# Block two of a two-block transformer: the first delta-rule chunk begun between dense products, and rotary embedding, blanks and decayed queries made by GpSimd

## The chip, the core and the metric

The kernel runs as one program on one core of a Trainium2 chip. The core has five engines that run side by side and wait for each other with semaphores: TensorE (PE: matmuls and transposes, into eight PSUM banks), VectorE (DVE), ScalarE (ACT), GpSimd (POOL) and SyncE (SP: here it only issues loads). The metric is the device time of one execution in microseconds (us); lower is better.

## The reference, cut to what matters

Two transformer blocks follow each other on 256 tokens of width 1024, all in float32. The change is in the second, whose mixer puts 16 meta tokens ahead of the 256 and runs two kinds of heads on one input projection:

```
proj = u @ w_in
dq, dk, dv, dz, db, da, aq, ak, av = split(proj)
# delta heads: 4 of width 128, forward and backward over the tokens
q, k, v = silu(short_conv([dq, dk, dv])); q, k = l2_norm(q) * 128**-0.5, l2_norm(k)
kk = k @ k.T ; a_low = strictly_lower(kk * decay * beta)
u, w = solve(a_low + I, [v * beta, k * beta * exp(gc)])
v_new = u - w @ S ; o = (q * exp(gc)) @ S + (q @ k.T * decay) @ v_new
S = S * g_last + k_dec.T @ v_new                # from chunk to chunk
# axial heads: 8 query heads on 2 key heads, width 64
q, k = rms_norm(aq) * q_norm, rms_norm(ak) * k_norm
x1, x2 -> x1 * cos - x2 * sin, x2 * cos + x1 * sin     # rotary embedding
o_at = softmax(q @ k.T / 8) @ av
mix = [rms_norm(o) * silu(dz), o_at] @ w_out
```

Then come a residual, a norm and an MLP. The reference's chunk of 64 is cut here into chunks of 16 (meta) and 128 tokens, which gives the same result.

## The kernel before

Every engine runs one long program, written out by Python in the order of the code; there is no scheduler and no loop on the chip. The order in which the functions `..._tensor`, `..._scalar`, `..._vector` and `..._gpsimd` call their operations is the order on that engine's queue, and the first instruction of a queue that waits holds back everything behind it. `then_inc(*vec.up(name))` tells that a result is there, `wait_ge(*vec.at(name))` waits for it.

**Dense products.** A weight chunk lands in a ring, ScalarE rounds it to a high part (`round_weights`, L515), VectorE subtracts for the low part (`lower_weights`, L521), and TensorE multiplies in three passes (L527 to L529). The input projection of block two is eleven such chunks, IN2 to IN2 + 10; the last four are `aq0`, `aq1` (queries of the axial heads), `z0`, `z1` (the gate dz), 48 matmuls each. This stage is called "two" (`in_tensor`, `in_scalar`, `in_vector`, `in_gpsimd`). `rows_tensor` and `rows_scalar` turn k (0) and v (1) of the delta heads to token order (`kv_tok`).

**Delta chunks.** A chunk is (d, t): direction d, token tile t, where t = 2 is the 16 meta tokens and t = 0, 1 are 128 tokens each. Six chunks run: (0,2), (1,2), (0,0), (1,1) from the start and (0,1), (1,0) from round 4. Each is a Python generator on each of three engines, and its steps are: sums of the gates ("gc"); the differences of their running sums ("R", which gives `d_a`, `d_qk` and `d_qdec`); k times k ("K", into `d_a`); the transpose of `d_a` and the first guess of its inverse `d_x`; then, for 128 tokens, six levels of two steps each that double the inverse (`d_w` from L2443, `d_x` from L2455 and L2457); and the products with q, v and the state S (names with `_last` are the buffers of (0,1) and (1,0), with `_meta` those of the meta chunks). One round of `beside_axial` takes one step of every chunk that lives and, between them, two steps (later one or two) of the axial heads.

**Rotary embedding.** The first steps of the axial heads prepare q and k of the token tiles t = 0, 1, 2: ScalarE squares (`sqk`, L2761), VectorE sums (L2818), ScalarE takes the root (L573, L575), VectorE scales and turns (`rotate_vector`, L2818 to L2847: 11 or 12 operations a tile into `rot`), TensorE transposes (L2710, L2714), ScalarE copies to `aT` and `akT`. After tile 2 the attention of the axial heads follows unit by unit.

**Dummy products.** `keep_running(e, n, ...)` puts n matmuls of the identity (L582) on TensorE's queue, whose result nobody reads.

## Time and profile before

| | us |
|---|---|
| median of 3 runs (lowest, highest) | 1154.88 (1152.62, 1156.89) |
| the profiled execution: device time | 1154.68 |
| the profiled execution: span from first to last instruction | 1152.9 |
| TensorE busy over the span | 1095.7 |
| VectorE busy | 761.2 |
| ScalarE busy | 608.9 |
| GpSimd busy | 65.5 |

The span is 1.8 us shorter than the device time of the same execution. "Busy" counts instructions in flight, so a busy TensorE can still be running at half its clock. The delta stage and the tail of stage "two" lie between 770 and 935 us of the span. A row of the timeline gives start, duration and count; of several instructions in a row the starts are closer together than the single duration, since the engine begins the next before the last has drained.

### The profile page before, as it was taken

How to read it: one execution, taken by the hardware profiler on the slowest of the kernel's cores; microseconds unless marked ns; L12 is line 12 of the kernel's file. 1: busy time of each engine (PE TensorE's matmuls, PEld its weight loads, DVE VectorE, ACT ScalarE, POOL GpSimd, SP SyncE). 2: the span in 40 equal slices, each digit the busy share in tenths (PEclk: the TensorE clock that was granted, in tenths of full speed). 3: DMA queues.
4: the chain of work that ended last, by engine and by line, in shares of the span. 5: the costliest groups of instructions: out<-in, count | busy, mean ns of one | idle time of the engine just before them, and what ended most of it. 6: DMA issues, size and time to landing. Idle time of an engine off the chain costs nothing.

```text
span 1152.9 us, 20471 instructions
## 1 busy us (share of the span) xinstructions
PE 1095.7 (95%) x8417; PEld 974.4 (85%) x8417; DVE 761.2 (66%) x1282; ACT 608.9 (53%) x1102; POOL 65.5 (6%) x84
## 2 busy tenths in 40 slices
PE   6999989999999999889999999998789999999997
PEld 3989567999899899879999988998668888999986
DVE  1786877899987775578655447874876557444443
ACT  2544756543544556656455555466664345565453
POOL 0012770000000000000000000110000000000000
PEclk8999999999999999999999999999789999999999
DMA  9997116899997354336856551250000045555540
GB/s 371 406 395 319 38 43 250 308 362 358 343 355 264 139 209 165 113 126 213 328 188 219 183 182 40 99 231 2 1 2 21 5 180 184 194 188 183 183 147 36
DMA packets 33564, 218.30 MB, mean 189 GB/s; under 512 B 4528, under 2 KB 5296, under 8 KB 8896
## 3 DMA queue, kind: packets, MB, share of 16 engines
q1 hardware_dynamic: 33472, 217.00, 50.9%
q8 instruction: 67, 1.10, 0.4%
q14 instruction: 25, 0.20, 0.0%
HBM read 215.93 MB, written 1.05 MB: 188 GB/s over the span
## 4 chain that ended last, share of the span: by engine, by line
PE 76%; DVE 11%; ACT 7%; DMA 2%; POOL 2%; issue 1%; DVEq 0%; SPq 0%; ACTq 0%
PE bank L527 20%; PE bank L529 20%; PE bank L528 20%; DVE low L521 2%; ACT high L515 2%; DMA ring<-ada_halves 2%; POOL zb L1141 1%; PE bank L567 1%; PE bank L644 1%; PE bank L2455 1%; PE bank L2457 1%; DVE y_tmp L1607 1%; PE bank L582 1%; PE bank L2443 1%; DVE stats L1609 1%
## 5 line engine op out<-in xcount | busy, mean ns | idle before, releaser
L521 DVE TENSOR_TENSOR low<-ring,high 128x2048 fp32r<-128x2048 f32 (+1 forms) x139 | 317.6, 2287 | 242.2 <-ACT high L515 241.8
L515 ACT ACTIVATE high<-ring 128x2048 fp32r<-128x2048 f32 (+1 forms) x139 | 264.7, 1906 | 247.5 <-PE bank L529 199.5
L527 PE MATMUL bank<-act_high,high 128*128 128x256 f32 (+1 forms) x1072 | 308.3, 288 | 0.0
L529 PE MATMUL bank<-act_high,low 128*128 128x256 f32 (+1 forms) x1072 | 303.8, 283 | 0.0
L528 PE MATMUL bank<-act_low,high 128*128 128x256 f32 (+1 forms) x1072 | 303.6, 283 | 0.0
L527 PE MATMUL bank<-high,act_high 128*128 128x512 f32 (+1 forms) x632 | 233.7, 370 | 3.2 <-DVE act_low L3005 1.8
L529 PE MATMUL bank<-high,act_low 128*128 128x512 f32 (+1 forms) x632 | 231.2, 366 | 0.0
L528 PE MATMUL bank<-low,act_high 128*128 128x512 f32 (+1 forms) x632 | 231.2, 366 | 0.0
L527 PEld LDWEIGHTS bank<-act_high,high 128*128 128x128 f32 x1072 | 205.0, 191 | 4.5 <-issue 2.4
L528 PEld LDWEIGHTS bank<-act_low,high 128*128 128x128 f32 x1072 | 205.0, 191 | 2.4 <-issue 1.4
L529 PEld LDWEIGHTS bank<-act_high,low 128*128 128x128 f32 x1072 | 204.9, 191 | 0.0
L527 PEld LDWEIGHTS bank<-high,act_high 128*128 128x128 f32 x632 | 119.5, 189 | 23.8 <-DVE act_low L3005 2.0
L529 PEld LDWEIGHTS bank<-high,act_low 128*128 128x128 f32 x632 | 119.2, 189 | 20.6
L528 PEld LDWEIGHTS bank<-low,act_high 128*128 128x128 f32 x632 | 119.4, 189 | 18.0
L626 DVE SCALAR_TENSOR_TENSOR ada_acc<-ring,c_act,ada_acc 128x512 f32<-128x512 f32 x105 | 79.4, 756 | 4.6
L1134 ACT ACTIVATE zb<-zb,ust 128x128 f32<-128x128 f32 x80 | 35.5, 446 | 27.1 <-DVE ust L1126 27.1
L582 PEld LDWEIGHTS bank<-cols 128*128 128x128 f32 x338 | 41.2, 200 | 4.9 <-issue 4.8
L582 PE MATMUL bank<-cols 128*128 128x128 f32 x338 | 43.3, 285 | 0.0
L1141 POOL TENSOR_SCALAR zb<-zb,ust 128x128 f32<-128x128 f32 (+1 forms) x48 | 40.2, 851 | 32.5 <-DVE ust L1414 24.7
L2352 POOL MEMSET conv<- 128x24 f32 x1 | 0.1, 123 | 538.8 <-DVE x_tok L2122 538.8
L1149 PE MATMUL bank<-cols,zb 128*128 128x128 f32 x96 | 16.4, 281 | 7.9 <-DVE zb L1954 2.4
L1149 PEld LDWEIGHTS bank<-cols,zb 128*128 128x128 f32 x96 | 10.6, 141 | 14.2 <-DVE zb L1954 2.6
(511 smaller groups left out, 1384.1 us busy)
## 6 DMA issues: line engine op xcount, KB each, us to landing
ring<-chunks SPq DMA_DIRECT2D x138, 1024.0 KB, 5.0
ring<-ada_halves SPq DMA_DIRECT2D x38, 1024.0 KB, 5.1
o_land<-ada_halves SPq DMA_DIRECT2D x6, 1024.0 KB, 11.9
ring<-raw_cmp SPq DMA_DIRECT2D x4, 1024.0 KB, 11.5
x_tok<-ada_halves SPq DMA_DIRECT2D x3, 1024.0 KB, 15.1
gate_rows<-ada_b SPq DMA_DIRECT2D x4, 512.0 KB, 9.9
bias<-bias_by_distance SPq DMA_DIRECT2D x1, 2048.0 KB, 13.2
ln_rows<-ln_g SPq DMA_DIRECT2D x4, 512.0 KB, 6.0
```

Of the source, the lines that this page charges most:

```text
L515: e.activation(weights(c)[0], in_ring(("w", c)), ACT.Copy).then_inc(*act.up("high", c))
L521: e.tensor_tensor(low, in_ring(("w", c)), high.bitcast(F32), ALU.subtract).then_inc(*vec.up("low", c))
L527: e.matmul(out_, ah, bh, start=start, stop=False)
L528: e.matmul(out_, ah, bl, start=False, stop=False)
L529: return e.matmul(out_, al, bh, start=False, stop=stop)
L567: last = e.matmul(out_, src[:, k, toks], w[:, k, c0:c0 + n_cols], start=k == 0, stop=k == n - 1)
L582: m = e.matmul(b[:, 0:P], ident, ident, start=True, stop=True)
L626: e.scalar_tensor_tensor(acc, w_[:, k, :], c_, acc, ALU.mult, ALU.add).then_inc(*vec.up("ada_op", l, j, i))
L644: m = e.matmul(b[:, i:i + 1], acc[:, i * P:(i + 1) * P], ones[:, 0:1], start=True, stop=True)
L1134: x = e.activation(z[:, c], z[:, c], ACT.Exp, bias=st[:, t:t + 1], scale=-1.0, accum_out=st[:, 2 + t:3 + t])
L1141: x = e.tensor_scalar(z[:, c], z[:, c], st[:, 4 + t:5 + t], None, ALU.mult)
L1149: m = e.transpose(b[:, tok(i)], z[:, tok(i)], ident)
```

## The change

- **First chunk ahead.** The generators of chunk (0,0) are made before stage "two" (`ahead`) and take their first four steps inside it: gc after `aq0`, R and K after `aq1`, the transpose of `d_a` after `z0`. `beside_axial` then goes on with step 5 of (0,0) in its round 0. On TensorE the turn of v (`rows_tensor(e, 1)`) moves behind `z1`; on ScalarE its copies (`rows_scalar(e, 1)`) move to the end of the stage, behind the table load.
- **Rotary embedding.** `rotate_vector` keeps the sum of the squares; the other operations of a tile go to GpSimd (`rotate_gpsimd`). The square and the sum of tile t + 1 are drawn forward to the fourth axial step of tile t, behind the end of tile t's rotation.
- **Blanks and decayed queries.** The `memset` of a quarter of `d_xT` and the product `d_qdec` times q of the four 128-token chunks leave VectorE for GpSimd.
- **Dummy products.** 20 ahead of tile 1's transposes are dropped; 12 in the first level of (0,2) become 6.

```diff
@@ in_tensor
-            for half in range(2):
-                rows_product(e, IN2 + 7 + half, f"aq{half}")
+            rows_product(e, IN2 + 7, "aq0")
+            steps_of(ahead, 1)
+            rows_product(e, IN2 + 8, "aq1")
+            steps_of(ahead, 2)
             rows_product(e, IN2 + 9, "z0")
             rows_tensor(e, 0)
+            steps_of(ahead, 1)
+            rows_product(e, IN2 + 10, "z1")
             rows_tensor(e, 1)
-            rows_product(e, IN2 + 10, "z1")
@@ in_scalar
                 if half == 0:
                     rows_scalar(e, 0)
-                    rows_scalar(e, 1)
+                    steps_of(ahead, 1)
                     round_weights(e, OUT2)
+                    steps_of(axial, 2)
             e.preload_act_table_set(ROOTS)
-            steps_of(axial, 2)
+            rows_scalar(e, 1)
@@ in_vector
             lower_weights(e, IN2 + 9)
+            steps_of(ahead, 2)
             lower_weights(e, IN2 + 10)
+            steps_of(axial, 1)
+            steps_of(ahead, 1)
             steps_of(axial, 2)
+            steps_of(ahead, 1)
             lower_weights(e, OUT2)
-            steps_of(axial, 2)
+            steps_of(axial, 1)
@@ in_gpsimd
+            rotate_gpsimd(e, 0)
+            blank_gpsimd(e, 0, 0)
+            rotate_gpsimd(e, 1)
+            blank_gpsimd(e, 1, 1)
+            rotate_gpsimd(e, 2)
+            for d in range(2):
+                decay_gpsimd(e, d, d)
+            for d in range(2):
+                blank_gpsimd(e, d, 1 - d)
+            for d in range(2):
+                decay_gpsimd(e, d, 1 - d)
@@ delta_tensor
-                keep_running(e, 12, "x", k)
+                keep_running(e, 6, "x", k)
@@ delta_scalar
+            if k == (0, 0):
+                e.activation(B["qk"], B["qk"], ACT.Exp).then_inc(*act.up("qk", k))
...
-            if real:
+            if real and k != (0, 0):
                 e.activation(B["qk"], B["qk"], ACT.Exp).then_inc(*act.up("qk", k))
@@ axial_tensor
-                    if t == 1:
-                        keep_running(e, 20, "rot", t)
-                    e.wait_ge(*vec.at("rot", t))
+                    e.wait_ge(*pool.at("rot", t))
@@ rotate_gpsimd (was rotate_vector; in the new order)
+            e.wait_ge(*act.at("rot_square", t))
+            if t < 2:
+                e.tensor_tensor(x_[:, 0:8, :], x_[:, 0:8, :], qk_norm_row[0:r, 0:1, :].broadcast_to([r, 8, 64]), ALU.mult)...
+            e.tensor_tensor(k_, k_, qk_norm_row[0:r, 1:2, :].broadcast_to([r, 2, 64]), ALU.mult)...
+            e.wait_ge(*act.at("rot_root", t))
+            e.tensor_tensor(k_, k_, rst[0:r, 1, 8:10].unsqueeze(2).broadcast_to([r, 2, 64]), ALU.mult)...
+            e.wait_ge(*vec.at("rot_sum", t))
+            e.tensor_tensor(tmp, hi_, sin, ALU.mult)...
+            e.tensor_tensor(tmp2, lo_, sin, ALU.mult)...
+            e.tensor_tensor(o_lo, lo_, cos, ALU.mult)...
+            e.tensor_tensor(o_hi, hi_, cos, ALU.mult)...
+            e.tensor_tensor(o_lo, o_lo, tmp, ALU.subtract)...
+            e.tensor_tensor(o_hi, o_hi, tmp2, ALU.add).then_inc(*pool.up("rot", t))
```

The three places below are where this shows in the order of the instructions; lines are those of each version's own file.

On VectorE, between the low part of `z1`'s weights (`low_61`) and the delta stage (its first row is `d_st` 16x4), before:

```order
L521 TENSOR_TENSOR low_61<-ring_55,high_59 128x2048 [waits scalar_two]
L2818 TENSOR_REDUCE rst<-sqk 128x10 [waits scalar_two]
L2820 TENSOR_TENSOR aqk<-aqk,qk_norm_row 128x512
...
L521 TENSOR_TENSOR low_62<-ring_56,high_60 128x2048 [waits scalar_two]
L2839 TENSOR_TENSOR rot<-aqk,rope 128x20x16 [waits vector_two]
...
L2847 TENSOR_TENSOR rot<-rot,sqk 128x20x16 [waits vector_two]
L2581 TENSOR_TENSOR d_st<-d_st 16x4 [waits scalar_delta,vector_two]
```

and now:

```order
L521 TENSOR_TENSOR low_61<-ring_55,high_59 128x2048 [waits scalar_two]
L2840 TENSOR_REDUCE rst<-sqk 128x10 [waits scalar_two]
L2625 SCALAR_TENSOR_TENSOR d_a<-bank,ba,d_a 128x128 [waits tensor_two,scalar_two]
...
L2631 TENSOR_TENSOR d_x<-d_a,masks 64x256 [waits vector_two]
...
L2636 TENSOR_TENSOR d_x<-d_aT,masks 64x256 [waits scalar_two]
...
L2639 TENSOR_TENSOR d_x<-masks,d_x 128x512 [waits vector_two]
L521 TENSOR_TENSOR low_62<-ring_56,high_60 128x2048 [waits scalar_two]
L2840 TENSOR_REDUCE rst<-sqk 128x10 [waits scalar_two]
L2607 TENSOR_TENSOR d_st<-d_st 16x4 [waits scalar_delta,vector_two]
```

The rotation is gone from the queue, chunk (0,0) has come into it, and the second sum (tile 1) stands ahead of the delta stage.

On ScalarE, from the copies of k (`kv_tok`) to the delta stage, before:

```order
L2186 ACTIVATE kv_tok<-bank 16x512 [waits tensor_two]
L2186 ACTIVATE kv_tok<-bank 128x512 [waits tensor_two] x2
L515 ACTIVATE high_60<-ring_56 128x2048 [waits tensor_two,in_ring1]
L2279 ACTIVATE z_tok<-bank 128x2x256 [waits tensor_two]
L2285 ACT_TABLE_LOAD
L2524 ACTIVATE d_st<-bank 16x4 [waits tensor_delta,scalar_two]
```

and now:

```order
L2567 ACTIVATE d_aT<-bank 128x512 [waits tensor_two]
L515 ACTIVATE high_60<-ring_56 128x2048 [waits tensor_two,in_ring1]
L2780 ACTIVATE sqk<-aqk 128x640 [waits gpsimd_two]
L2286 ACTIVATE z_tok<-bank 128x2x256 [waits tensor_two]
L2293 ACT_TABLE_LOAD
L2186 ACTIVATE kv_tok<-bank 16x512 [waits tensor_two]
L2186 ACTIVATE kv_tok<-bank 128x512 [waits tensor_two] x2
L2548 ACTIVATE d_st<-bank 16x4 [waits tensor_delta,scalar_two]
```

The copies of v now stand between the table load and the delta stage, and tile 1's square, which waits for GpSimd's rotation of tile 0, stands ahead of `z1`'s copy.

On TensorE, in round 2 of the delta stage around tile 1's transposes, before:

```order
L582 MATMUL bank<-cols 128x128 [waits scalar_delta]
L582 MATMUL bank<-cols 128x128 x19
L2710 MATMUL bank<-cols,rot 128x128 [waits vector_delta,scalar_delta]
...
L2714 MATMUL bank<-cols,rot 128x128 [waits vector_delta,scalar_delta]
L2424 MATMUL bank<-cT 128x128 [waits vector_two,scalar_delta]
...
L2430 MATMUL bank<-cols,d_a_meta 16x16 [waits vector_delta,scalar_delta]
```

and now:

```order
L2466 MATMUL bank<-d_x,d_aT 64x64 [waits vector_delta]
...
L2730 MATMUL bank<-cols,rot 128x128 [waits gpsimd_two,scalar_delta]
...
L2734 MATMUL bank<-cols,rot 128x128 [waits gpsimd_two,scalar_delta]
L2447 MATMUL bank<-cT 128x128 [waits vector_two,scalar_delta]
...
L2453 MATMUL bank<-cols,d_a_meta 16x16 [waits vector_delta]
```

The dummy products are gone, chunk (0,0) is already at its second level (L2466), and the transposes wait for GpSimd.

## Rows read from the trace of the kernel before

**Rows 1.** Five stretches: length; busy us of each engine; granted TensorE clock; DMA.

```profile
core 0: us, PE busy (x) PEld busy (x) DVE busy (x) ACT busy (x) POOL busy (x), PEclk, DMA share, GB/s
797.40:829.40 32.00, 21.16 (x203) 19.48 (x202) 26.15 (x90) 21.42 (x71) 0.00 (x0) 0.84 0.00 1
829.40:842.00 12.60, 12.53 (x155) 11.10 (x155) 6.53 (x28) 9.27 (x38) 0.00 (x0) 0.60 0.01 1
842.00:862.00 20.00, 14.51 (x275) 12.02 (x274) 15.77 (x51) 12.61 (x38) 0.00 (x0) 0.95 0.01 3
862.00:867.00 5.00, 5.00 (x78) 4.14 (x80) 3.06 (x11) 2.05 (x6) 0.00 (x0) 0.51 0.00 0
867.00:935.00 68.00, 67.44 (x1085) 59.49 (x1086) 37.47 (x91) 27.45 (x84) 0.00 (x0) 1.00 0.13 42
```

**Rows 2.** TensorE's timeline: start, us, line, operation, count, idle time before.

```profile
770.34 0.48 PE L527 MATMUL bank<-high,act_high 128*128 128x256 f32 x1
...
790.30 1.47 PE L2179 MATMUL bank<-cols,cT 128*16 128x128 f32 x12 [1.22 <-ACT cT L2242]
...
800.30 0.63 PE L2710 MATMUL bank<-cols,rot 128*128 128x128 f32 x4 [2.41 <-DVE rot L2847]
...
809.65 4.63 PE L582 MATMUL bank<-cols 128*128 128x128 f32 x40
816.92 0.63 PE L2710 MATMUL bank<-cols,rot 128*128 128x128 f32 x4 [2.64 <-DVE d_a_meta L2599]
...
817.49 1.06 PE L2424 MATMUL bank<-cT 128*128 128x128 f32 x8
...
872.62 1.15 PE L2443 MATMUL bank<-d_x,d_aT 64*64 64x64 f32 x32
```

**Rows 3.** VectorE's groups in 797.4 to 829.4: line, shapes, count, busy us, mean ns.

```profile
L2588 DVE SCALAR_TENSOR_TENSOR d_a<-bank,d_st,masks 128x128 f32<-128x128 f32 x8 | 2.6, 329 | 0.0
L2612 DVE TENSOR_TENSOR d_x<-d_aT,masks 64x256 f32<-64x256 f32 x4 | 1.7, 420 | 0.1
L2843 DVE TENSOR_TENSOR rot<-rot,sqk 128x320 f32<-128x320 f32 x2 | 1.0, 478 | 0.0
```

**Rows 4.** VectorE's timeline.

```profile
777.07 0.18 DVE L2343 TENSOR_TENSOR ba<-ba,ex_row 128x24 f32<-128x24 f32 x1
...
828.62 0.69 DVE L2615 TENSOR_TENSOR d_x<-masks,d_x 128x512 f32<-128x512 f32 x1
...
855.84 0.87 DVE L2612 TENSOR_TENSOR d_x_last<-d_aT_last,masks 64x256 f32<-64x256 f32 x2 [2.21 <-ACT d_aT_last L2541]
```

**Rows 5.** ScalarE's timeline.

```profile
784.62 0.74 ACT L2761 ACTIVATE sqk<-aqk 128x640 f32<-128x640 f32 x1
...
790.54 2.95 ACT L2186 ACTIVATE kv_tok<-bank 16x512 f32<-16x512 f32 x6
...
797.49 0.60 ACT L2279 ACTIVATE z_tok<-bank 128x512 f32<-128x512 f32 x1 [2.20 <-PE bank L529]
798.11 1.28 ACT L2285 ACT_TABLE_LOAD   x1
799.40 0.16 ACT L2524 ACTIVATE d_st<-bank 16x4 f32<-16x4 f32 x1
...
808.04 0.21 ACT L575 ACTIVATE rst<-rst 128x10 f32<-128x10 f32 x1
...
852.90 2.43 ACT L2519 ACTIVATE d_kdec<-kv_tok,d_st 128x128 f32<-128x128 f32 x8
```

**Rows 6.** Single lines: GpSimd's products and VectorE's low parts; ns min/median/max.

```profile
L1064 POOL TENSOR_TENSOR hid<-hid 128x120 f32<-128x120 f32 x1 | 0.4, 389 | 29.2 <-ACT hid L903 29.2
...
L1495 POOL TENSOR_TENSOR dbias<-bias,taken x8: 720/726/2697, 138.4 to 164.9; 128x256 f32<-128x256 f32 x8
...
L2357 POOL TENSOR_TENSOR conv<-cT x8: 640/642/2752, 738.5 to 755.9; 128x272 f32<-128x272 f32 x8
...
L521 DVE TENSOR_TENSOR low<-ring,high x11: 2279/2293/2574, 720.0 to 795.3; 128x2048 fp32r<-128x2048 f32 x11
```

More of the change, by code:

```diff
@@ L2187, in rows_scalar, with in_tensor @@
                     *act.up("kv_tok", kv, t))
-        def in_tensor(e, axial):
+        def in_tensor(e, axial, ahead):
             for t in range(QT):
@@ L2344, in in_vector @@
             lower_weights(e, IN2 + 9)
+            steps_of(ahead, 2)
             lower_weights(e, IN2 + 10)
+            steps_of(axial, 1)
+            steps_of(ahead, 1)
             steps_of(axial, 2)
+            steps_of(ahead, 1)
             lower_weights(e, OUT2)
-            steps_of(axial, 2)
+            steps_of(axial, 1)
         def in_gpsimd(e):
@@ L2466, in delta_tensor @@
                 e.wait_ge(*act.at("rows", k))
+                e.wait_ge(*pool.at("blank", k))
                 e.wait_ge(*vec.at("xT", k, n_levels - 1))
@@ L2605, in delta_vector @@
                 e.tensor_tensor(xs[r, 0:4, :], B["a"][r, :, r], level(0, 1 - back, r), ALU.mult).then_inc(*vec.up())
-            if real:
-                e.memset(B["xT"][far, :, near], 0.0).then_inc(*vec.up())
             if k == (0, 2):
@@ L2672, in program, with beside_axial @@
         CHUNKS = (((0, 2), 0), ((1, 2), 0), ((0, 0), 0), ((1, 1), 0), ((0, 1), 4), ((1, 0), 4))
-        def beside_axial(chunks, axial):
+        def beside_axial(chunks, axial, ahead):
             live, waiting, n = [], list(CHUNKS), 0
@@ L2678, in beside_axial @@
                 for k, start in [c for c in waiting if c[1] == n]:
-                    live.append(chunks(*k, k[1] == 2 or k[0] == k[1]))
+                    live.append(ahead if k == (0, 0) else chunks(*k, k[1] == 2 or k[0] == k[1]))
                 waiting = [c for c in waiting if c[1] > n]
@@ L2756, in axial_scalar, with square @@
         def axial_scalar(e):
+            def square(t):
+                r, h0 = TT_ROWS[t], 0 if t < 2 else 8
+                e.wait_ge(*(pool.at("rot", t - 1) if t else act.at("aq1")))
+                e.activation(sqk[0:r, h0:10, :], aqk[0:r, t, h0:10, :], ACT.Square).then_inc(*act.up("rot_square", t))
             for t in range(3):
-                r = TT_ROWS[t]
-                h0 = 0 if t < 2 else 8
-                e.wait_ge(*(vec.at("rot", t - 1) if t else act.at("aq1")))
-                e.activation(sqk[0:r, h0:10, :], aqk[0:r, t, h0:10, :], ACT.Square).then_inc(*act.up("rot_square", t))
+                r, h0 = TT_ROWS[t], 0 if t < 2 else 8
+                if t == 0:
+                    square(t)
                 yield
@@ L2766, in axial_scalar @@
                 yield
+                if t < 2:
+                    square(t + 1)
                 yield
@@ L2813, in rotate_vector, with blank_gpsimd, decay_gpsimd, rotate_gpsimd @@
             r, h0 = TT_ROWS[t], 0 if t < 2 else 8
+            e.wait_ge(*act.at("rot_square", t))
+            e.tensor_reduce(rst[0:r, 0, h0:10], sqk[0:r, h0:10, :], AX_X, ALU.add).then_inc(*vec.up("rot_sum", t))
+        def blank_gpsimd(e, d, t):
+            back = d
+            e.wait_ge(*pool.now())
+            e.wait_ge(*act.at("w", (d, t)))
+            e.memset(buf[d, t]["xT"][HALVES[1 - back], :, HALVES[back]], 0.0).then_inc(*pool.up("blank", (d, t)))
+        def decay_gpsimd(e, d, t):
+            B = buf[d, t]
+            e.wait_ge(*pool.now())
+            e.wait_ge(*act.at("qdec", (d, t)))
+            e.tensor_tensor(B["qdec"], B["qdec"], cT[:, 0:4, rows_of(t)], ALU.mult).then_inc(*pool.up("qdec", (d, t)))
+        def rotate_gpsimd(e, t):
+            r, h0 = TT_ROWS[t], 0 if t < 2 else 8
             x_, sq_ = aqk[0:r, t, h0:10, :], sqk[0:r, h0:10, :]
@@ L3036, in tensor @@
             pe.stage("two")
-            axial = axial_tensor(e)
-            in_tensor(e, axial)
+            axial, ahead = axial_tensor(e), delta_tensor(e, 0, 0, True)
+            in_tensor(e, axial, ahead)
             pe.stage("delta")
-            beside_axial(lambda *chunk: delta_tensor(e, *chunk), axial)
+            beside_axial(lambda *chunk: delta_tensor(e, *chunk), axial, ahead)
             pe.stage("end")
@@ L3062, in scalar @@
             act.stage("two")
-            axial = axial_scalar(e)
-            in_scalar(e, axial)
+            axial, ahead = axial_scalar(e), delta_scalar(e, 0, 0, True)
+            in_scalar(e, axial, ahead)
             e.wait_ge(*act.now())
             act.stage("delta")
-            beside_axial(lambda *chunk: delta_scalar(e, *chunk), axial)
+            beside_axial(lambda *chunk: delta_scalar(e, *chunk), axial, ahead)
             e.wait_ge(*act.now())
@@ L3092, in vector @@
             vec.stage("two")
-            axial = axial_vector(e)
-            in_vector(e, axial)
+            axial, ahead = axial_vector(e), delta_vector(e, 0, 0, True)
+            in_vector(e, axial, ahead)
             e.wait_ge(*vec.now())
             vec.stage("delta")
-            beside_axial(lambda *chunk: delta_vector(e, *chunk), axial)
+            beside_axial(lambda *chunk: delta_vector(e, *chunk), axial, ahead)
             e.wait_ge(*vec.now())
```

56 lines of the change are left out of this document (29 added, 27 removed).

## The prediction

> **What bounds the kernel now.** The page gives a busy TensorE for nearly the whole span, so the first thing to find is where it is not the limit. I read the windows first, stage by stage, then TensorE's timeline for the waits in them, then the queues of the engines that it waits for. From 867 to 935 us TensorE is busy 67.4 of 68.0 us at full clock: there the time is TensorE's work [rows 1]. From 797.4 to 829.4 it is different: TensorE counts as busy 21.2 of 32 us, and that includes 20 dummy products (4.6 us) and 12 more; VectorE is busy 26.2 us of the 32 [rows 1, 2]. TensorE waits there 2.4 us for tile 0's rotation (800.30) and 2.6 us ahead of tile 1's transposes (816.92) [rows 2]. So this stretch is VectorE's, and its end is the first guess of chunk (1,1), 828.62 + 0.69 = 829.3 [rows 4]. After it, up to 842, TensorE is the limit at mostly half its clock (0.60), and from 842 to 862 waits alternate with work: 14.5 of 20 us busy, with VectorE held 2.2 us by ScalarE at 855.84 [rows 1, 4]. The change works on the VectorE stretch, on that wait, and on the amount of work in TensorE's stretch.
>
> **What goes from VectorE.** In 797.4 to 829.4 the six products of a rotation take 1.0 us for two calls each (tiles 0 and 1), 5.9 us in all; tile 2 and the scalings of tiles 1 and 2 are some 2.5 more. Chunk (0,0)'s share in that stretch is half of the groups of `d_a`, `d_qk` and `d_x`: 4 of 8 at 0.33 for each of three kinds and 2 of 4 at 0.42 for each of two, 0.7 for the last, together 6.3 us [rows 3]. What comes in is two levels of (0,0), about 2.2 us. VectorE's 26.2 us become about 14, so it no longer sets the pace there. The blanks (64x256, below the 0.42 us of a product of that shape) and the decayed queries lie where TensorE is the limit or behind this slack; I give them nothing.
>
> **What it costs in stage "two".** `aq0` starts at 770.34; `z1`, a product of the same size, ran from 791.8 (790.30 + 1.47) to 797.4, where ScalarE's copy is let go, so a product takes some 5.7 us and `aq0` ends at 776.05 [rows 2, 5]. The gate sums behind it need `ba`, which VectorE ends at 777.25 [rows 4]: TensorE waits 1.3 us. Then, with matmuls at 1.06 us for eight instructions (817.49): gc 0.5, `aq1` 5.7, R and K 2.1, `z0` 5.7, the turn of k 1.5, the transpose 0.6 (as at 816.92), `z1` 5.7 [rows 2]. The end is 799.2 instead of 797.4: of the 4.5 us put in, 1.2 are paid by the wait at 790.30 that goes, and 1.5 by the turn of v that moves behind. Behind `z1` ScalarE now has its copy (0.6), the table load (1.28) and the three copies of v (half of 2.95) before the meta chunk may begin: 799.3 + 3.4 = 802.7, and 803.3 for ScalarE's first row of the delta stage, which was at 799.40 [rows 5]. The head thus starts **3.9 us later**.
>
> **GpSimd's price.** The trace has no rotation on GpSimd. Its two-input products of 120 and 256 columns take 0.39 and 0.72 us [rows 6]: 0.1 us plus 2.4 ns a column, so 0.88 us for 320 columns, 1.34 for 512, 0.41 for 128. Lower bound: the 0.64 us of 272 columns where both inputs are one tensor, 0.75 for 320. Upper bound: the longest row, 2.75 us, a product that met VectorE's low part [rows 6]. I take the fit, since no low part runs beside most of the products. A rotation is 1.8 us ahead of the root and 5.8 behind it. Tile 0: its square ended at 785.4 and moves with `aq1` by 1.6 us, so GpSimd begins at 787.0, beside a low part that runs to 789.2, and ends at 797 to 798. What waits for it first is tile 1's square, ahead of `z1`'s copy on ScalarE, and that copy can't start before 799.2: the rotation and the 0.7 us of the square are just covered. Tile 1: its root stood 8.8 us behind ScalarE's first row of the stage (799.40 to 808.25) [rows 5]; less one set of gate sums and the wait for VectorE, plus 1.2 us of copies for (0,0), I make it 7.4 us, 810.7. GpSimd ends at **816.5**. Nothing covers this one: the square of tile 2 waits for it on ScalarE, the sum behind that on VectorE, and the transposes with everything behind them on TensorE.
>
> **The new head.** From 816.5: transposes 0.9, K of (1,1) 1.1, its `d_a` 1.2 (four at 0.33 each, less overlap), the low part 2.3, the meta chunks' guesses 1.5 (six small operations of a quarter us, an estimate), one level of (0,0) 0.7, the first guess of (1,1) 2.5 [rows 2 to 4, 6]. This gives 826.7 against 829.3, **2.6 us earlier**. Against it stand the decayed queries: two products of 1.3 us that fall beside that first guess on the same operand ports, and a TensorE that may run at half clock there since the 20 dummies are gone. Both together cost between 0 and 3 us; I take 0.8, since most of the guess's operations are short. Term one: **-1.8**.
>
> **Behind the head.** At 852.90 ScalarE makes eight `d_kdec` copies (2.43 us) ahead of the transpose copy that VectorE waits for at 855.84 [rows 4, 5]. Four of them, (0,0)'s, are then long done: 1.2 us, and 0.3 for a blank on VectorE's side of the same chain. Term two: **-1.5** (0 to -2).
>
> In TensorE's stretch, (0,0) is four steps further, so two levels of it have left it. A level is 16 instructions for `d_w` (32 take 1.15 us at 872.62) and 32 for `d_x`, 1.6 us [rows 2]. Two are 3.2 us less work where TensorE is the limit; some of it will be lost to waits when fewer chunks live, so term three is **-2.6** (0 to -3.2).
>
> **Loads and queues.** No load is moved. The rounding of the two output weight chunks shifts by +2 and about -2 us, which shifts the loads that wait for their ring slots; DMA share is 0.00 to 0.13 there [rows 1], so that is hidden.
>
> **Sum.** -1.8 - 1.5 - 2.6 = -5.9 us. The profiled execution took 1154.7 us, 0.2 below the median of the runs shown, so the forecast is **1148.8 us**, 0.5% below that median, the size that a measurement of this kernel can just tell from no change.
>
> **Rivals.**
> 1. *GpSimd sets the pace of the head.* For: GpSimd's products of 272 columns are 0.64 us, but 2.75 us when one meets a low part, whose own longest is 2.57 instead of 2.29 [rows 6]; the six products read short runs of 16, which no row shows; nothing hides tile 1. Against: VectorE is mostly idle in 811 to 816. At the mean over the eight (1.17 us for 272 columns) the six products take 8.3 us instead of 5.3, with the scalings 3.8 us more; the head then gains nothing, and the time is 1148.8 + 3.8 = 1152.6. The Trainium skill, "SBUF — State Buffer", section "Who interferes with whom", says that a VectorE instruction with two SBUF inputs and a GpSimd instruction that reads SBUF exclude each other, the later one waiting for the whole of the other. The rows agree: 2752 against 640 ns, beside a low part of 2293.
> 2. *The clock holds better.* 829.4 to 842 and 862 to 867 are at 0.60 and 0.51 of the clock [rows 1], both behind idle time of TensorE that the change shortens; chunk (0,0)'s levels now fill the head. If 5 us of work at half clock run at full, another 3.5 us go: 1145.3. Against it: the dummies are gone.
> 3. *Slower: the clock is lost.* Of 32 dummy products 6 are left. Before, the 20 ran from 809.65 [rows 2] in the middle of a stretch at 0.84 [rows 1]. If TensorE is at half clock through the head and does not get the full one back between 842 and 862, its 14.5 us of work there become 29 in a stretch of 20: some 8 us more, and 3 in the head for transposes, R, K and their like. -5.9 + 11 = +5: 1160. It decides when more than 6 us of full-clock work turn to half clock; in the rows before, the full clock came back by itself at 842.
> 4. *Nothing comes of it.* The head gains what stage "two" lost, and the two levels taken out of the tail leave waits of the same length, as the last chunks (0,1) and (1,0) start in the same round as before: 1154.5. Against it: 67.4 of 68.0 us busy.
>
> **How the numbers follow.** Forecast 0.44 (own range 1146 to 1152, of which about half lies below the bound of 0.5%), rival 1 0.22, rival 2 0.20, rival 3 0.08, rival 4 0.06. Faster by over 0.5%: rival 2 and somewhat over half of the forecast, 0.46; slower by over 0.5%: most of rival 3 and the far end of rival 1 (both rotations late by 10 us or more), 0.10; the rest, 0.44, within it. The range that leaves out 2 in 10 reaches from the middle of rival 2 to beyond rival 4: 1143 to 1156.5.
>
> **What would show it.** In the changed trace: `z1` ends near 799.2 and ScalarE's first delta row stands near 803.3; GpSimd's products of 320 columns take 0.75 to 1.0 us; tile 1's rotation ends near 816.5 and the sum of tile 2 on VectorE right behind it; the first guess of (1,1) ends near 827.5; the stretch from there to the end of the delta stage is some 4 us shorter than the 105.7 us of before (829.3 to 935). The forecast is wrong in its core if tile 1's transposes wait for GpSimd beyond 820, or if the stage's granted clock is below that of before.

## The result and the profile after

The changed kernel takes **1148.36 us** (median of 4 runs, 1147.47 to 1150.43), the kernel before in the same comparison 1155.25 (1152.62 to 1156.89): a ratio of 0.9941, 95% interval 0.992 to 0.9962. A second comparison, run beside experiments 5 to 7, gave 1146.36 against 1153.97, 0.9927 (0.9908 to 0.9945). What was expected of it:

> The changed kernel once more, beside the others on one chip. Its runs so far spread over 3 us, and in the runs of all kernels the time falls by about 0.7 us for each 0.001 that the mean granted clock is higher. Theory (three terms, the head's worth less than forecast): 1147 to 1149, a ratio of 0.993 to 0.995, and about 7.5 us below the kernel before at the same granted clock. Rival (the first measurement was lucky): 1150 or more.

The change is faster by 0.6 to 0.7%. The forecast was 1148.8 us.

The page of the changed kernel gives VectorE 752.8 us (66%) instead of 761.2, and GpSimd 96.3 instead of 65.5. TensorE's sum moves only from 1095.7 to 1093.3. The five stretches of [rows 1], in the execution that was profiled (1150.43 us, span 1148.6, the slowest of the four):

```profile
core 0: us, PE busy (x) PEld busy (x) DVE busy (x) ACT busy (x) POOL busy (x), PEclk, DMA share, GB/s
797.40:829.40 32.00, 21.10 (x252) 19.04 (x250) 20.82 (x56) 22.39 (x73) 17.03 (x23) 0.77 0.00 1
829.40:842.00 12.60, 12.10 (x155) 10.54 (x155) 5.66 (x21) 8.10 (x34) 0.61 (x2) 0.64 0.01 3
842.00:862.00 20.00, 15.84 (x292) 12.83 (x292) 15.79 (x52) 11.45 (x34) 2.54 (x2) 0.92 0.01 2
862.00:867.00 5.00, 5.00 (x94) 4.54 (x92) 2.56 (x10) 2.43 (x7) 0.00 (x0) 0.62 0.02 3
867.00:935.00 68.00, 68.00 (x982) 59.71 (x978) 36.39 (x87) 27.69 (x85) 0.00 (x0) 0.97 0.19 63
```

In the first stretch VectorE has gone from 26.15 to 20.82 us and is no longer the engine that fills it; GpSimd has 17.03. The granted clock there is 0.77, where before had 0.84. GpSimd's timeline there (start, us, engine, line, operation; in brackets the idle time before it and what ended it):

```profile
787.78 3.03 POOL L2863 TENSOR_TENSOR aqk<-aqk,qk_norm_row 128x512 f32<-128x512 f32 x1 [29.74 <-ACT sqk L2780]
...
810.37 0.40 POOL L2868 TENSOR_TENSOR aqk<-aqk,rst 128x128 f32<-128x128 f32 x1 [8.09 <-ACT rst L575]
...
810.95 0.87 POOL L2879 TENSOR_TENSOR sqk<-aqk,rope 128x320 f32<-128x320 f32 x1
...
815.20 0.86 POOL L2887 TENSOR_TENSOR rot<-rot,sqk 128x320 f32<-128x320 f32 x1
...
825.49 2.73 POOL L2852 TENSOR_TENSOR d_qdec<-d_qdec,cT 128x512 f32<-128x512 f32 x2
```

TensorE's timeline of the same stretch:

```profile
803.00 0.19 PE L2434 MATMUL bank<-ba,masks 16*16 16x4 f32 x2 [2.43 <-ACT kv_tok L2186]
...
816.21 1.09 PE L2730 MATMUL bank<-cols,rot 128*128 128x128 f32 x4 [3.79 <-POOL rot L2887]
...
817.30 1.92 PE L2447 MATMUL bank<-cT 128*128 128x128 f32 x8
...
829.37 1.12 PE L2466 MATMUL bank<-d_x,d_aT 64*64 64x64 f32 x16 [3.65 <-DVE d_w_meta L2650]
```

And VectorE's: its last row on the gates, then the two guesses, and the last sum of the delta stage:

```profile
777.67 0.18 DVE L2351 TENSOR_TENSOR ba<-ba,ex_row 128x24 f32<-128x24 f32 x1
...
825.73 2.77 DVE L2636 TENSOR_TENSOR d_x<-d_aT,masks 64x256 f32<-64x256 f32 x2
828.53 0.69 DVE L2639 TENSOR_TENSOR d_x<-masks,d_x 128x512 f32<-128x512 f32 x1
...
854.58 0.87 DVE L2636 TENSOR_TENSOR d_x_last<-d_aT_last,masks 64x256 f32<-64x256 f32 x2 [1.31 <-ACT d_aT_last L2567]
...
930.91 0.69 DVE L2680 TENSOR_TENSOR o_acc<-o_acc,bank 128x512 f32<-128x512 f32 x1 [1.10 <-PE bank L2517]
```

The reader is to see three things. The rotation of tile 1 ends at 816.06 and TensorE goes on at 816.21, having waited 3.79 us for it. Then `L2636`, which took 0.87 us in [rows 4], takes 2.77, and it lies beside GpSimd's decays (825.49 to 828.22). Last, the first guess of (1,1) ends at 829.22, nearly where it did (829.31).

**A common clock for the comparison.** The gates end at another time in each execution (773.4 to 778.5 us over the kernels below), in code that the change does not touch. So all traces are compared from the start of VectorE's last row on the gates (777.67 above): "head" is from there to the end of the first guess of (1,1), "middle" to the end of the last first guess of the last chunks, "tail" to the end of the last `o_acc` sum. What is left after that is 217.0 us in every trace (216.98 to 217.10). Times are worked out from rows like those above.

| kernel | median us | ratio (95%) | head | middle | tail | tail's clock | tail's TensorE instructions |
|---|---|---|---|---|---|---|---|
| before | 1155.25 | 1 | 52.24 | 30.91 | 75.62 | 0.96 | 1188 |
| changed | 1148.36 | 0.9941 (0.992 to 0.9962) | 51.55 | 29.36 | 73.02 | 0.93 | 1092 |
| changed, again | 1146.36 | 0.9927 (0.9908 to 0.9945) | 52.03 | 28.51 | 68.73 | 1.00 | 1092 |
| 1 decays moved | 1147.56 | 0.9934 (0.9916 to 0.9952) | 49.72 | 29.37 | 73.01 | 0.93 | 1092 |
| 2 root early | 1148.00 | 0.9931 (0.991 to 0.9952) | 51.21 | 28.79 | 71.22 | 0.96 | 1092 |
| 3 GpSimd's part only | 1151.11 | 0.9966 (0.9949 to 0.9982) | 51.29 | 30.12 | 74.58 | 0.96 | 1188 |
| 4 chunk ahead only | 1150.00 | 0.9957 (0.9939 to 0.9976) | 52.22 | 29.75 | 70.13 | 0.98 | 1092 |
| 5 dummies back | 1147.08 | 0.9933 (0.9915 to 0.995) | 51.96 | 28.68 | 71.16 | 0.96 | 1092 |
| 6 three moves | 1144.30 | 0.9918 (0.99 to 0.9936) | 47.30 | 29.09 | 72.84 | 0.93 | 1092 |
| 6 again | 1144.20 | 0.9905 (0.9887 to 0.9923) | 47.31 | 29.22 | 72.90 | 0.93 | 1092 |
| 7 moves and dummies | 1143.79 | 0.9921 (0.9895 to 0.9947) | 47.29 | 28.86 | 72.61 | 0.98 | 1122 |
| 8 low part later | 1144.64 | 0.991 (0.9895 to 0.9926) | 45.53 | 30.50 | 72.93 | 0.93 | 1092 |

The tail of one and the same kernel is 73.02 us in one execution and 68.73 in another, at a granted clock of 0.93 and 1.00. Length times clock is the same within 1 us: 67.9 and 68.7 (the clock has two digits, so such a product is good to some 0.4 us). Read that way, the kernels with the chunk ahead have 67.7 to 68.7 us of full-clock tail, and those without it 72.6 (before) and 71.6 (experiment 3). Experiment 7 stands apart with 71.2, as 30 more instructions lie in its tail.

### The profile page after: what moved, and what is told of

Read it like the earlier page. It is cut to its first block, busy times and chain, and to the rows that moved or that the text cites. A ratio compares the mean times of both kernels' runs of the same rounds, so it can differ in the third digit from the quotient of the medians.

```text
span 1148.6 us, 20388 instructions
## 1 busy us (share of the span) xinstructions
PE 1093.3 (95%) x8365; PEld 973.4 (85%) x8365; DVE 752.8 (66%) x1246; ACT 609.1 (53%) x1102; POOL 96.3 (8%) x120
## 4 chain that ended last, share of the span: by engine, by line
PE 77%; DVE 9%; ACT 7%; DMA 2%; POOL 2%; issue 1%; DVEq 0%; SPq 0%; ACTq 0%; POOLq 0%
PE bank L527 20%; PE bank L529 20%; PE bank L528 20%; DVE low L521 2%; ACT high L515 2%; DMA ring<-ada_halves 2%; POOL zb L1141 1%; PE bank L567 1%; PE bank L2478 1%; PE bank L644 1%; PE bank L2480 1%; PE bank L582 1%; DVE y_tmp L1607 1%; DMA ring<-raw_ksv 1%; DVE stats L1609 1%
## 5 line engine op out<-in xcount | busy, mean ns | idle before, releaser
L582 PEld LDWEIGHTS bank<-cols 128*128 128x128 f32 x286 | 36.2, 206 | 4.3 <-issue 4.2
L582 PE MATMUL bank<-cols 128*128 128x128 f32 x286 | 38.2, 291 | 0.0
```

The lines of the kernel that those rows point to most:

```text
L582: m = e.matmul(b[:, 0:P], ident, ident, start=True, stop=True)
```

## The experiments

**1. The decays elsewhere.** GpSimd makes the decayed queries of (0,0) ahead of tile 1's rotation and those of (1,1) ahead of tile 2's.

```diff
             blank_gpsimd(e, 0, 0)
+            decay_gpsimd(e, 0, 0)
             rotate_gpsimd(e, 1)
             blank_gpsimd(e, 1, 1)
+            decay_gpsimd(e, 1, 1)
             rotate_gpsimd(e, 2)
-            for d in range(2):
-                decay_gpsimd(e, d, d)
```

> The changed kernel with the decayed queries of (0,0) made by GpSimd ahead of tile 1's rotation and those of (1,1) ahead of tile 2's, instead of behind tile 2's. Theory (port): the decays, two products in 2.73 us at 825.49, stretched VectorE's L2636 at 825.73 from 0.87 to 2.77 us; moved away, that row is 0.9 to 1.5 again, the first guess of (1,1) ends 1.9 us earlier than 829.2, TensorE's wait of 3.65 us ahead of it shrinks by as much, and the time is 1.9 below that of the changed kernel, 1146.5 (ratio to before 0.9925). Rival (clock): TensorE at half clock or another wait sets the place; the row is short but the next level starts no earlier, and the time stays at 1148.4. Second rival: the product of (0,0) now meets VectorE's low part at 798.5 and pushes tile 1's rotation beyond 816; the time is 1149 or more.

VectorE's timeline of that kernel, at the guess:

```profile
824.54 0.87 DVE L2636 TENSOR_TENSOR d_x<-d_aT,masks 64x256 f32<-64x256 f32 x2
825.45 0.69 DVE L2639 TENSOR_TENSOR d_x<-masks,d_x 128x512 f32<-128x512 f32 x1
```

and TensorE's row behind it:

```profile
826.29 1.12 PE L2466 MATMUL bank<-d_x,d_aT 64*64 64x64 f32 x16 [1.75 <-DVE d_w_meta L2650]
```

The row is 0.87 us again, the head is 49.72 instead of 51.55 (1.83 less; 2.3 less than in the second trace), and TensorE's wait has gone from 3.65 to 1.75. The middle is as long as in the changed kernel's first trace (29.37 and 29.36); head and middle together are 1.8 us shorter than there and 1.5 shorter than in the second, so the gain is kept: the port theory holds, and the two rivals fall. The Trainium skill, "SBUF — State Buffer", section "Who interferes with whom", has the rule: a VectorE instruction with two SBUF inputs and a GpSimd instruction that reads SBUF don't run together, and the later one waits for the whole of the other. The traces agree: 2.77 us beside the decays, 0.87 without. The time of the whole (1147.56 against 1148.36 and 1146.36) can't tell 1.9 us.

**2. Tile 1's root early.** `root` is the wait for the sum and the two operations of the root, taken out of `axial_scalar`.

```diff
@@ in_scalar
             rows_scalar(e, 1)
+            root(e, 1)
@@ axial_scalar
-                e.wait_ge(*vec.at("rot_sum", t))
-                rsqrt(e, rst[0:r, 1, h0:10], rst[0:r, 0, h0:10], 1.0 / 64, eps6, "rot_root", t)
+                if t != 1:
+                    root(e, t)
```

> The changed kernel with the root of tile 1 (two operations on ScalarE) right behind the copies of v, ahead of the delta stage, instead of at 809.77. Theory (nothing covers tile 1): GpSimd has waited 8.1 us for that root; its rotation of tile 1 now ends near 809 instead of 816.1, TensorE's wait of 3.8 us at 816.2 is gone, and K of (1,1) comes at about 815. VectorE then still stands at tile 2's sum until 816.7, as ScalarE's square of tile 2 is behind the rounding of an output chunk; so of the 7 us only 1.5 reach the first guess of (1,1): 827.7, and a time of 1146.9 (ratio 0.9928). Rival (clock): the rotation comes early, but the first guess of (1,1) stays at 829.2 because it waits for products at half clock; 1148.4. Second rival: all of it arrives, the first guess ends 4 us earlier, 1144.5.

ScalarE's timeline of that kernel around tile 2's square:

```profile
812.65 0.60 ACT L2564 ACTIVATE d_qdec<-bank 128x512 f32<-128x512 f32 x1 [2.40 <-DVE d_qk L2623]
813.14 0.62 ACT L2565 ACTIVATE d_a<-d_a 128x512 f32<-128x512 f32 x1
813.66 1.90 ACT L515 ACTIVATE high<-ring 128x2048 fp32r<-128x2048 f32 x1
815.46 0.29 ACT L2786 ACTIVATE sqk<-aqk 16x128 f32<-16x128 f32 x1
```

and VectorE's row that waits for it:

```profile
815.78 0.27 DVE L2846 TENSOR_REDUCE rst<-sqk 16x2 f32<-16x128 f32 x1 [2.62 <-ACT sqk L2786]
```

The rotation of tile 1 ended at 806.85, 9.2 us earlier (7 from the gates), and TensorE made the transposes at 811.48 without a wait. The head gained 0.3 us (0.8 against the second trace), less than the 1.5 expected. One wait of the head did go. In the changed kernel VectorE waited 1.47 us (1.19 in its second trace) for K of (1,1), which TensorE makes behind tile 1's transposes:

```profile
819.32 1.13 DVE L2625 SCALAR_TENSOR_TENSOR d_a<-bank,ba,d_a 128x128 f32<-128x128 f32 x4 [1.47 <-PE bank L2447]
```

In experiment 2 the same row has no wait:

```profile
816.88 1.10 DVE L2631 SCALAR_TENSOR_TENSOR d_a<-bank,ba,d_a 128x128 f32<-128x128 f32 x4
```

So the rotation held the head by 1.2 to 1.5 us, as expected. Ahead of that wait a second chain ran beside it, nearly as long: VectorE's `d_a` and `d_qk`, ScalarE's exponentials, the rounding of an output chunk (1.90 us), tile 2's square, tile 2's sum. This chain came later in experiment 2: the sum began 40.20 us behind the gates, instead of 39.01 and 39.76 in the changed kernel's two traces. The early rotation (801.18 to 806.85) now lies beside VectorE's small gate sums:

```profile
801.88 0.76 DVE L2613 TENSOR_TENSOR d_st<-d_st 16x4 f32<-16x4 f32 x1 [2.50 <-ACT d_st L2556]
803.00 0.46 DVE L2615 TENSOR_TENSOR d_st<-d_st,ba 16x4 f32<-16x4 f32 x1 [0.37 <-ACT d_st L2560]
```

In the changed kernel they took 0.15 us each:

```profile
803.97 0.15 DVE L2607 TENSOR_TENSOR d_st<-d_st 16x4 f32<-16x4 f32 x1 [2.49 <-ACT d_st L2550]
```

This took back 0.4 to 1.2 us of the gain. That the ports are the reason here too is argued from experiment 1; no run moved these sums away from the rotation.

**3 and 4. One half of the change each.** The third kernel is the kernel before with the GpSimd part alone, the fourth with the first chunk ahead alone; both keep the 32 dummy products.

```diff
@@ experiment 3, against the kernel before
+            rotate_gpsimd(e, 0)
...
-                    e.wait_ge(*vec.at("rot", t))
+                    e.wait_ge(*pool.at("rot", t))
@@ experiment 4, against the kernel before
-            axial = axial_tensor(e)
-            in_tensor(e, axial)
+            axial, ahead = axial_tensor(e), delta_tensor(e, 0, 0, True)
+            in_tensor(e, axial, ahead)
...
+            steps_of(ahead, 1)
```

> The kernel before with only the rotation, the blanks and the decayed queries given to GpSimd; chunk (0,0) is not begun ahead, and the dummy products stay. Theory (three terms): terms two and three belong to the chunk that is begun ahead, so only the head can gain. It starts as before, at 799.4; tile 1's rotation ends near 814.5 instead of 816.9; with the decays on the same ports as the guesses the head gains 0.5 to 2.5 us and the stretch behind it is as long as before (105.7): 1153.5 (ratio 0.9987, 0.998 to 1.000). Rival: the whole gain is GpSimd's, VectorE's 26 us being the bound of the stretch; then the time is that of the changed kernel, 1148.5 (0.994).

> The kernel before with only chunk (0,0) begun between the dense products; rotation, blanks and decayed queries stay on VectorE, and the dummy products stay. Theory (three terms): the head starts 3.9 us later (803.3) and has 4.1 us less for VectorE (6.3 out, 2.2 of two levels in), so its first guess of (1,1) ends near 829.1, where it did; behind it terms two and three are there as in the changed kernel, 1.6 and 2.6 us; 1150.9 (ratio 0.9963). Rival (GpSimd is needed): VectorE's rotation of tile 0 and (0,0)'s steps get in each other's way in stage two, the copy of z1 and the head come 3 us or more later still, and the time is that of before or above (1.000 to 1.004).

The chunk ahead alone gives 0.9957: head 52.22 (expected: as before), middle 1.16 us shorter, 96 instructions fewer in the tail, which is 68.7 us at full clock instead of 72.6. That is its theory; the rival that it needs GpSimd falls. GpSimd's part alone gives 0.9966, more than expected: 1.0 us in the head, as expected, but also 0.8 in the middle and 1.0 in the tail. The rows tell where they lie. Among what has left VectorE's queue are the blank between its last two guesses and the decayed queries of the last chunks; before they stood there:

```profile
858.33 0.27 DVE L2607 MEMSET d_xT_last<- 64x256 f32 x1
...
886.17 0.68 DVE L2628 TENSOR_TENSOR d_qdec_last<-d_qdec_last,cT 128x512 f32<-128x512 f32 x1
```

Without the blank, VectorE's step from one of these guesses to the next is 0.89 us instead of 1.27, 0.4 of the 0.8. Behind the decayed queries, VectorE's sum of `d_x` comes 1.0 us earlier from the start of the tail instead of the 0.6 that TensorE was already ahead, 0.5 of the 1.0. The rest, 0.4 in the middle and 0.6 in the tail, lies where TensorE's half clock ends earlier (16 products of R take 2.05 us instead of 2.61, at 838.5); whether the change or chance did that is open. The two halves make 0.34 and 0.43%, together 0.77%; the whole change has 0.59 and 0.73%. They add up within the intervals.

**5. The dummy products back.**

```diff
@@ delta_tensor
-                keep_running(e, 6, "x", k)
+                keep_running(e, 12, "x", k)
@@ axial_tensor
+                    if t == 1:
+                        keep_running(e, 20, "rot", t)
```

> The changed kernel with the dummy products of before restored: 20 ahead of tile 1's transposes, 12 instead of 6 at chunk (0,2). In the changed kernel TensorE is idle for 3.8 us ahead of 816.2 and the transposes and K of (1,1) behind that run at half clock (1.92 us for K). Theory (forecast's step: the clock costs less than 1 us in the head): the 20 products take 4.6 us at full clock and end 0.9 us after the rotation, transposes and K are 1.4 us shorter, the first guess of (1,1) ends within 0.7 us of 829.2, the time is within 1 us of the changed kernel. Rival 3 of the forecast (the clock is lost without them): the head's granted clock rises from 0.77 to 0.85 or more, the first guess ends 2 us or more earlier, and the time is 1146 or less. Rival (they run at half clock): 9 us of dummies, the first guess ends 5 us later, 1153.

TensorE's timeline of that kernel:

```profile
812.18 4.73 PE L582 MATMUL bank<-cols 128*128 128x128 f32 x40
816.75 0.60 PE L2732 MATMUL bank<-cols,rot 128*128 128x128 f32 x4
...
817.30 1.06 PE L2447 MATMUL bank<-cT 128*128 128x128 f32 x8
```

K of (1,1) takes 1.06 us instead of 1.92, the transposes 0.60 instead of 1.09, as they run at the full clock: the two are done in 1.6 us instead of 3.0. But the 4.73 us of dummies end 1.7 us later than the rotation did (816.91 against 815.24), and so K ends 41.95 us behind the gates, where the changed kernel has 41.55 and 42.01. The head is 51.96, between the two traces of the changed kernel, and the time 1147.08. Dropping the dummies neither cost nor gave anything. That is no price of the half clock: this run buys the full clock with a wait as long as what it saves, and no run has the one without the other.

**6. Three moves in the head.** The moves of 1 and 2, and the rounding of the output chunk one chunk later in ScalarE's round, behind tile 2's square:

```diff
@@ delta_scalar
-            if k == (0, 2):
+            if k == (1, 2):
                 round_weights(e, OUT2 + 1)
```

> The changed kernel with three moves in its head: the decays as in the first experiment, tile 1's root behind the copies of v as in the second, and the rounding of the output chunk on ScalarE one chunk later, behind tile 2's square, which stood behind it for 1.9 us. Theory (the head is a chain over ScalarE, GpSimd and VectorE, and what it gains is kept): 1.8 us from the decays, 0.4 from the root, 1.5 to 1.9 from the rounding; measured from the end of the gates the first guess of (1,1) ends 3.5 to 4.2 us earlier than in the changed kernel, and the time is 1144 to 1145 (ratio 0.990 to 0.991). Rival (the rounding only moves the wait): the low part of the same chunk comes 1.9 us later on VectorE and stands ahead of the guess as before, the head gains 2.2 us, 1146. Rival (the half clock behind the head takes it back): 1147.5 or more.

VectorE's timeline of that kernel (gates at 777.42):

```profile
816.12 0.27 DVE L2846 TENSOR_REDUCE rst<-sqk 16x2 f32<-16x128 f32 x1 [0.82 <-ACT sqk L2786]
...
817.22 1.10 DVE L2631 SCALAR_TENSOR_TENSOR d_a<-bank,ba,d_a 128x128 f32<-128x128 f32 x4
...
818.38 2.27 DVE L521 TENSOR_TENSOR low<-ring,high 128x2048 fp32r<-128x2048 f32 x1
...
823.11 0.89 DVE L2642 TENSOR_TENSOR d_x<-d_aT,masks 64x256 f32<-64x256 f32 x2
824.03 0.69 DVE L2645 TENSOR_TENSOR d_x<-masks,d_x 128x512 f32<-128x512 f32 x1
```

The wait for the square is 0.82 instead of 2.62 us, the low part begins 40.96 us behind the gates instead of 42.82, so the rival falls, and the head is 47.30: 4.25 us less than in the changed kernel (4.73 against its second trace), where 3.5 to 4.2 were expected. The middle is no longer for it (29.09), so the gain is kept. Experiments 1 and 2 have 1.83 and 0.34 of the 4.25; the rounding, which was not moved alone, is left with some 2.1 by subtraction. Run a second time, it repeats to 0.1 us in the head; the expectation of that run stands here beside the next one's.

> The kernel with the three moves once more, beside the one above on one chip. Theory: behind the gates 47.3 us to the first guess of (1,1) and about 29 more to the last first guess again, since these stretches have varied by 1 us or less between executions of one kernel; a ratio of 0.990 to 0.992. Rival (the better time was scatter of the granted clock): 0.993 or more.

The ratios, 0.9918 and 0.9905, are below both of the changed kernel; the interval of the second ends at 0.9923, below the changed kernel's 0.9927 and 0.9941, though the intervals of the changed kernel reach down to 0.9908. In the one comparison that had both kernels, 1144.30 stands against 1146.36 with intervals that overlap: the gain in the head is shown by the traces, and in the time it is likely and no more.

**7. Dummy products in three waits.**

```diff
@@ delta_tensor
+        DUMMIES = {(0, 2): 6, (1, 1): 7, (0, 1): 4, (1, 0): 7}
...
-            if k == (0, 2):
-                keep_running(e, 6, "x", k)
+            if k in DUMMIES:
+                keep_running(e, DUMMIES[k], "x", k)
```

> The kernel with the three moves, and dummy products in three waits of TensorE: 7 ahead of the first level of (1,1), 4 ahead of that of (0,1), 7 ahead of that of (1,0), where it is idle for 1.75, 0.9 and 1.75 us and the granted clock falls to half within 2 us behind, for 6 to 8 us. Theory (the clock falls because of these waits): the half-clock stretches behind them shrink, 3 to 7 us of time come back on top of the three moves, and the mean granted clock rises by 0.003 or more: 1138 to 1142. Rival (the waits' length isn't what decides; the kernel before had 12 such products there and fell to half clock all the same): the stretches stay, the dummies cost 0 to 2 us, 1144 to 1147.

The mean granted clock of its runs is 0.983 against 0.979 in experiment 6; but the changed kernel without such products had 0.982 in the same comparison, so a rise can't be told from scatter. The time is 1143.79 against 1144.30: no gain. TensorE's rows of that kernel show what the products of the last two waits cost:

```profile
847.21 1.16 PE L582 MATMUL bank<-cols 128*128 128x128 f32 x8 [0.17 <-ACT d_aT_last L2575]
850.37 1.12 PE L2474 MATMUL bank<-d_x_last,d_aT_last 64*64 64x64 f32 x16 [2.00 <-DVE d_w_meta L2658]
851.42 2.90 PE L582 MATMUL bank<-cols 128*128 128x128 f32 x14
854.24 0.68 PE L2474 MATMUL bank<-d_x_last,d_aT_last 64*64 64x64 f32 x16
```

The guess of (0,1) ends at 847.79, but its level starts at 850.37, 2.6 us later; in experiment 6 it was 0.14. It waits for a row of VectorE that empties PSUM banks:

```profile
850.11 0.34 DVE L2658 TENSOR_TENSOR d_w_meta<-bank,masks 16x64 f32<-16x64 f32 x2
```

By the code, every `keep_running` takes a PSUM bank, so the products behind it get another bank of the ring than before, one that is not yet free. That is read from the code and the releaser, not tested. The products of (1,0) stand behind this, at half clock (14 in 2.90 us), and the level of (1,0) starts at their end, 4 us behind its guess (850.19), where experiment 6 has 0.17. At (1,1), the end of the head, the products too end 1.65 us behind the guess (822.98 against 821.33). Length times clock of this tail is 71.2 instead of 67.7: what the clock of 0.98 gave, the products and the later level took. The theory's 3 to 7 us did not come; how much of the half clock is owed to these waits stays open, as this run does not fill them without making them longer.

**8. The low part behind the guess.**

```diff
@@ delta_vector
-            if k == (0, 2):
-                lower_weights(e, OUT2 + 1)
             e.wait_ge(*act.at("aT", k))
...
                 *vec.up("x", k, 0))
             vec.also("xT", k, 0)
+            if k == (1, 1):
+                lower_weights(e, OUT2 + 1)
```

> The kernel with the three moves, and on VectorE the low part of the output chunk (2.27 us, which stands ahead of the first guesses) put behind the first guess of (1,1). Theory (the head's chain ends on VectorE, ScalarE close behind): the first guess can't start before ScalarE's copy of d_aT, which ended 1.3 us ahead of it, so it ends 1.0 to 1.3 us earlier (46.0 to 46.3 us behind the gates instead of 47.3); the gate sums of (0,1), which wait for the low part, come at about the time that they did, so of this gain half stays: 1143.8 (ratio 0.991). Rival (the work behind the guess pays): the masked products of (0,0) and the meta chunks now stand behind the low part, TensorE waits there for the 1 us that the guess gained, and the last first guess comes when it did: no change, within 0.3 us of 76.4 behind the gates.

The head falls to 45.53, by 1.8 us. The middle grows from 29.1 or 29.2 to 30.50, and the time stays (1144.64 against 1144.20). TensorE's rows of that kernel:

```profile
820.53 1.12 PE L2472 MATMUL bank<-d_x,d_aT 64*64 64x64 f32 x16 [1.85 <-DVE d_x L2643]
822.86 0.56 PE L2440 MATMUL bank<-ba,masks 128*128 128x4 f32 x2 [1.21 <-DVE d_w_meta L2656]
```

Behind the first level TensorE now waits 1.21 us more, for the gate sums of (0,1), which need the low part (820.31 + 2.40). Of 1.8 us 0.4 to 0.5 are left at the last first guess, not measurable in the time. The rival is nearly right: the wait has moved.

## Why the forecast was right, and where its steps were off

**The sum was right, two of its terms were not.** Forecast -5.9 us; measured -6.9 and -7.6 in the medians, and -4.8 in the first trace (head, middle and tail together), whose tail ran at 0.93 of the clock. That the sum came out is in part luck: term one was 1.1 to 1.6 us too large and term three, at equal clock, 1.3 to 2.1 too small.

**Stage "two"** went as worked out: the last product of `z1` ends at 799.26 (forecast 799.2), ScalarE's first delta row stands at 803.59 (803.3), GpSimd's products of 320 columns take 0.87 us (0.88, from the two rows of [rows 6]), tile 1's rotation ends at 816.06 (816.5). Of VectorE's time in the stretch, "about 14" us were forecast and 20.82 measured. Of the 6.8 us between, 2.1 are a low part that now lies inside it (798.47; 795.33 before), 1.9 the row that met the decays and 1.1 a guess row of (0,0); the rest was not followed.

**Term one (-1.8): the step that failed is the 0.8 us for the decays and the half clock.** From 816.5 the forecast counted to 826.7, and with the 0.8 to 827.5; measured is 829.22. The rotation ended 0.4 earlier. Transposes and K ended 3.2 us behind it instead of 2.0, at half clock (819.22). From there to the first guess of (1,1) the count was right, 5.6 instead of 5.7. The guess itself took 4.4 instead of 2.5 (824.82 to 829.22), as its row met the decays; experiment 1 measures these alone at 1.8 to 2.3 us. Together that is 3.1 us where 0.8 was taken, at the top of the forecast's own 0 to 3, and it eats the 2.6 of the head whole: 829.22 against 829.31. The 0.7 us in the table's first trace is there because its gates ended 0.6 later; the second trace has 0.2. The forecast reasoned that "most of the guess's operations are short"; but a short operation that meets a product of 1.27 us waits for the product, not for its own length. The forecast's own [rows 6] had shown the same the other way round, a GpSimd product beside a low part (2752 against 640 ns).

**Term one, its other sentence.** "Nothing covers this one", said of tile 1's rotation, is half right: experiment 2 ended it 7 us earlier, and 1.2 to 1.5 us of VectorE's wait went with it. ScalarE's chain to tile 2's square covered the rest.

**Term two (-1.5): right, in both its parts.** ScalarE now makes four of the `d_kdec` copies in 1.26 us (852.81) where [rows 5] had eight in 2.43, VectorE waits 1.31 instead of 2.21 at the place of [rows 4], and the middle is 1.55 us shorter (2.4 in the second trace). The chunk ahead alone gives 1.16 (1.2 was forecast), and the blank that goes 0.38 (0.3; experiment 3).

**Term three (-2.6): the mechanism right, the size too small.** Here are the two tails, before:

```profile
860.22:935.84 75.62, 74.88 (x1188) 65.77 (x1189) 43.00 (x109) 29.50 (x90) 0.00 (x0) 0.96 0.13 42
```

and after:

```profile
858.58:931.60 73.02, 72.84 (x1092) 63.79 (x1093) 38.76 (x101) 29.62 (x90) 0.00 (x0) 0.93 0.13 43
```

1188 less 1092 is 96, exactly the two levels of 48 that were counted. Idle time of TensorE did not grow, as the 0.6 us taken off for waits assumed; it fell from 0.74 to 0.18. Two levels at 1.6 and 0.56 of idle are -3.8; the traces give -3.9 to -4.7 at equal clock (72.6 against 67.9 and 68.7). Experiment 4, which has the chunk ahead and nothing else, gives -3.9 alone. That the first trace's tail is 2.60 us shorter, just as forecast, is luck: its clock was 0.93 and that of before 0.96.

**The rivals.** Rival 1, GpSimd sets the pace: its mechanism came, at another place. Tile 1's rotation ran at the forecast's price. The low parts met three products: 3.03 us at 787.78 and 2.96 at 798.91, which nothing waited for, and one of tile 2's rotation, of 128 columns, which took 1.59 us instead of some 0.4 (821.43) and put the decays off by some 1.2. The decays were what the head paid for. Rival 2, the clock holds better: 829.4 to 842 rose from 0.60 to 0.64 and 862 to 867 from 0.51 to 0.62, little. The second trace had the tail at 1.00, but tails with the chunk ahead lie anywhere from 0.93 to 1.00, so that is scatter between executions. Rival 3, the clock is lost: 842 to 862, where it wanted half clock, had 0.92, and the time with the dummies back is the same. Rival 4, nothing: ruled out by both intervals, which end below 1, and in the tail by the idle time of TensorE, which did not grow with 96 instructions less.

**One sign misled.** The forecast called itself wrong in its core "if the stage's granted clock is below that of before". It was: 0.77 in the first stretch (0.74 in the second trace) against 0.84. Over the whole delta stage (797.4 to 935) it was 0.88 against 0.90, and 0.91 in the second trace. The time came out all the same: what the rows show of its cost in this stretch is the 1.2 us of transposes and K above. Of the other signs, the first guess missed 827.5 by 1.7 us, and the way from there to the end of the delta stage, 102.4 us instead of 106.5, is the forecast's 4 shorter.

## What to carry to other kernels

Work given to GpSimd is not free where VectorE is waited for: look at which two-input operations of VectorE fall beside it, and put GpSimd's long products where VectorE makes sums of one tile, reads a PSUM bank, or waits. Beside GpSimd's products here the sums of a tile's squares took 0.81 and 0.82 us, as before, and the `d_a` and `d_qk` rows, which read a bank, 0.34 to 0.35 (0.33 before); gate sums, with two inputs in SBUF, grew from 0.15 to as much as 0.76 us in experiment 2. Where a step ends 7 us earlier and the whole gains half a microsecond, follow the other input of the next instruction: in a round-robin of chunks a second chain can be nearly as long, and here a 1.9 us rounding of weights for a later stage stood in it. Work taken out of a stretch where one engine is busy throughout came off one for one here (3.9 us for two levels of 1.6 and 0.56 of idle time); count instructions in the two traces to see it.

## What was not expected of the hardware

Two executions of the changed kernel were 9 us apart (1150.43 and 1141.41 us), with the same instructions: 4.3 us lay ahead of the gates' end (777.67 against 773.35) and 4.3 in the tail (73.02 against 68.73). In both places the first has the lower granted clock: 0.98 against 1.00 from 400 to 600 us and from 700 to 773, 0.93 against 1.00 in the tail. Over the runs of the kernel before, the time goes with the mean granted clock: 1158.41 us at 0.975, 1151.87 at 0.987. The time of this kernel, whose TensorE is nearly always busy, is therefore known to some 2 us from six runs, and stages of one trace tell more than its total, if length times clock is compared and not the length.
